# First two up-projection blocks of each MLP as a pair with a seven-product group, and every up pair's group moved to quad 3

## The reference

```
def sq_relu_mlp(h, w_up, w_down):
    return jnp.square(jax.nn.relu(h @ w_up)) @ w_down

for l in range(DEPTH):                      # DEPTH = 2
    ... attention, x = x + ...
    x = x + sq_relu_mlp(rms_norm(x, mlp_norm_g[l]), w_up[l], w_down[l])
```

## Time and profile before

| | |
|---|---|
| median of 3 runs | 1978.41 us |
| profiled execution | 1977.89 us |
| its span, first to last instruction | 1975.9 us |
| mean granted TensorE clock | 0.999 of full speed |
| busy: TensorE, its weight loads, VectorE, ScalarE | 100%, 83%, 85%, 62% |
| mean DMA rate | 212 GB/s |

### The profile page before, as it was taken

One profiled execution on the slowest core, in us unless ns is written; L12 is line 12 of the kernel. 1 busy time (PEld: TensorE's weight loads), 2 busy tenths in 40 slices (PEclk: granted clock), 3 DMA queues, 4 the chain that ended last, 5 costly groups with the idle time before them and its releaser, 6 DMA issues.

```text
span 1975.9 us, 24462 instructions
## 1 busy us (share of the span) xinstructions
PE 1966.4 (100%) x9068; PEld 1639.2 (83%) x9068; DVE 1679.9 (85%) x2053; ACT 1229.9 (62%) x1579; POOL 34.3 (2%) x45
## 2 busy tenths in 40 slices
PE   9999999999999999999999999999999999999998
PEld 7888888888888888888888998888888888888887
DVE  7789997878988998898886787977998898898886
ACT  6555555656667566656656665656566666666663
POOL 0000000000000000000000000000000000000000
PEclk9999999999999999999999999999999999999999
DMA  8655546766787587677666554676587678658663
GB/s 304 217 171 184 178 169 198 232 203 215 224 242 232 190 242 241 211 232 225 224 219 208 147 152 138 224 237 224 188 230 239 226 226 240 210 204 256 216 233 117
DMA packets 269406, 418.23 MB, mean 212 GB/s; under 512 B 18801, under 2 KB 88817, under 8 KB 269297
## 3 DMA queue, kind: packets, MB, share of 16 engines
q1 hardware_dynamic: 262800, 401.06, 62.2%
q0 software_dynamic: 3456, 12.58, 3.5%
q10 hardware_dynamic: 3040, 3.15, 0.5%
HBM read 379.00 MB, written 2.10 MB: 193 GB/s over the span
## 4 chain that ended last, share of the span: by engine, by line
PE 97%; issue 2%; DVE 0%; ACT 0%; POOL 0%; POOLq 0%; DVEq 0%; ACTq 0%
PE acc L622 23%; PE acc L624 23%; PE acc L623 23%; PE side L821 3%; PE side L822 3%; PE side L820 3%; PE acc L820 3%; PE acc L822 3%; PE acc L821 2%; PE acc L642 2%; PE acc L643 2%; PE acc L644 2%; PE acc L980 1%; PE acc L982 1%; PE acc L981 1%
## 5 line engine op out<-in xcount | busy, mean ns | idle before, releaser
L1127 ACT ACTIVATE whi<-raw 128x1024 fp32r<-128x1024 f32 x556 | 570.1, 1045 | 319.6 <-PE acc L624 251.7
L1774 DVE TENSOR_TENSOR wlo<-raw,whi 128x1024 fp32r<-128x1024 f32 x556 | 659.1, 1204 | 108.8 <-ACT whi L1127 107.2
L622 PE MATMUL acc<-whi,opA 128*128 128x512 f32 (+2 forms) x1072 | 414.8, 387 | 0.0
L624 PE MATMUL acc<-whi,opA 128*128 128x512 f32 (+2 forms) x1072 | 414.0, 386 | 0.0
L623 PE MATMUL acc<-wlo,opA 128*128 128x512 f32 (+2 forms) x1072 | 413.8, 386 | 0.0
L622 PE MATMUL acc<-whi,opB 128*128 128x512 f32 x944 | 368.7, 391 | 0.0
L624 PE MATMUL acc<-whi,opB 128*128 128x512 f32 x944 | 367.6, 389 | 0.0
L623 PE MATMUL acc<-wlo,opB 128*128 128x512 f32 x944 | 367.3, 389 | 0.0
L624 PEld LDWEIGHTS acc<-whi,opA 128*128 128x128 f32 x1072 | 201.3, 188 | 40.3
L622 PEld LDWEIGHTS acc<-whi,opA 128*128 128x128 f32 x1072 | 201.3, 188 | 40.1 <-issue 0.3
L623 PEld LDWEIGHTS acc<-wlo,opA 128*128 128x128 f32 x1072 | 201.4, 188 | 40.0
(11 more groups left out here) (385 smaller groups left out, 2824.6 us busy)
## 6 DMA issues: line engine op xcount, KB each, us to landing
raw<-in_w_up SPq DMA_DIRECT2D x128, 1024.0 KB, 6.0
raw<-in_w_down SPq DMA_DIRECT2D x128, 1024.0 KB, 5.1
raw<-in_a_w_qkv SPq DMA_DIRECT2D x44, 1024.0 KB, 5.1
prob<-o_sb SPq DMA_DIRECT2D x168, 128.0 KB, 2.6
raw<-in_a_w_o SPq DMA_DIRECT2D x16, 1024.0 KB, 5.1
raw<-in_b_w_o SPq DMA_DIRECT2D x16, 1024.0 KB, 5.1
raw<-in_w_ukv SPq DMA_DIRECT2D x32, 256.0 KB, 4.1
xs<-junk POOLq DMA_DIRECT2D x12, 512.0 KB, 5.5
```

Of the source, the lines that this page charges most:

```text
L622: mm(o, a_hi, w_hi, start=start, stop=False)
L624: done = mm(o, a_lo, w_hi, start=False, stop=last and c == chunks - 1)
L1127: done = fn(whi[:, place:place + ch, 0:n], raw[:, r, c0:c0 + ch, 0:n], ACT.Copy)
L1774: done = tt_(wlo[:, place:place + ch, 0:n], raw[:, r, c0:c0 + ch, 0:n], whi[:, place:place + ch, 0:n].bitcast(F32), ALU.subtract)
```

## The change

The first two up blocks of each MLP become a pair, ("up", l, 0, 0), with a group of its own. The groups of all up pairs work on quad 3 (`opA` chunks 12 to 15) in place of quad 0, and the `x_forms` are made from those chunks. The later up pairs keep their order of slots, halves and forms; only which rows of the weights are loaded into which slot changes. The new first pair has another order than they: on TensorE six halves of block 0 (quads 0 to 2), four halves of block 1 (quads 0 and 1), the group, and then the last two halves of block 1 (quad 2).

More of the change, by code:

```diff
@@ L893, in up_pair @@
                     for hf in range(6):
-                        half_tok(b, hf, 1, chunks_of(opA, 4 + 2 * hf), first=hf == 0, uses=uses[1])
+                        half_tok(b, hf, 1, chunks_of(opA, 2 * hf), first=hf == 0, uses=uses[1])
                     shares_free(SHARE["up", l, q, i])
                     pe.wait_ge(form_lo, FORM_SETS * l + 2)
-                    seven(GROUP["up", l, q, i], b, 6, opA, 0, x_forms, uses[0], True, SHARED + ("B21", "T4"))
+                    seven(GROUP["up", l, q, i], b, 6, opA, 12, x_forms, uses[0], True, SHARED + ("B21", "T4"))
                     for hf in range(6):
-                        half_tok(b + 1, hf + 2, 0, chunks_of(opA, 4 + 2 * hf), first=hf == 0, last=hf == 5, uses=uses[0],
+                        half_tok(b + 1, hf + 2, 0, chunks_of(opA, 2 * hf), first=hf == 0, last=hf == 5, uses=uses[0],
                                  starts=(False, True))
-                for j in range(2):
-                    block_tok(B_MLP[l] + j, 1 - j, u[1 - j], opA, ready=None if j else opA_ready(v_in))
+                def up_first():
[12 more added lines that the diff above has]
+                        half_tok(b + 1, hf, 0, chunks_of(opA, 2 * hf - 4), last=hf == 7)
+                up_first()
                 up_pair(0, 1)
@@ L1441, in hid_high @@
                        ACT.Copy).then_inc(hid_hi, 1)
[L1443 to L1449, removed]
                 def turn_order(sums):
@@ L1550, in last_gains @@
                     act.dma_start(g_high, final_norm_g[D // 2:D].partition_broadcast(P)).then_inc(g_high_in, 16)
[L1552 to L1555, removed]
-                up_pair(0, 1, "plain")
+                def up_first():
[16 more added lines that the diff above has]
+                    split(b + 2, 2)
+                up_first()
+                up_pair(0, 1, "up")
                 for q in range(QUARTERS - 1):
@@ L2316, in sum_first @@
                     dve.wait_ge(shared_sums, 4 * SHARE["up", l, q, i] + 3)
-                    dve.wait_ge(sq_moves, 64 * (JB * (QUARTERS * l + q) + 2 * i))
+                    if l or q or i:
+                        dve.wait_ge(sq_moves, 64 * (JB * (QUARTERS * l + q) + 2 * i))
                     if q and i == 0:
@@ L2450, in up_pair @@
                         split(b + 2, hf)
-                body(B_MLP[l], {7: lambda: x_lo(v_in + JB - 1, G_MLP[l]), 8: lambda: stream_stats(2 * l + 1, True),
-                                9: x_form_sums})
-                body(B_MLP[l] + 1, {3: lambda: up_turn(0, 0), 4: lambda: form_low(x_forms, FORM_SETS * l + 1), 6: lambda: hid_low(0, 0)})
-                up_pair(0, 1, "plain")
+                def up_first():
[17 more added lines that the diff above has]
+                    split(b + 2, 2)
+                up_first()
+                up_pair(0, 1, "up")
                 for q in range(QUARTERS - 1):
```

## The result

The changed kernel took 1993.34 us (median of 6 runs, 1992.19 to 1993.79) against 1978.3 us before (6 runs): a ratio of 1.0076, 95% interval 1.0066 to 1.0087, slower by 15 us. Its profiled execution took 1993.43 us over a span of 1991.6 us, 15.54 us above that of before. The time is 1.6 us above the forecast of 1991.7.

A forecast was written before the change was run, and what follows sets the result against it. TensorE, without gaps, was taken as the bound. Per MLP 4.8 + 3.0 - 1.15 = 6.65 us, twice 13.3, on the profiled 1977.89 gives 1991.2; 0.52 more for the runs' median makes 1991.7, range 1985.0 to 1997.5.

The forecast's parts named there:

- The bound: TensorE runs matmul after matmul between the first blocks and the end, so any new wait is added in full.
- The gain of a group: On TensorE, each MLP swaps four halves (10.89 us) for a group (9.74 us): 1.15 us less.
- Up to the new group: VectorE delivers everything up to the new group in time, the tightest form by 0.4 us: counted as 0.
- The first stall: TensorE waits 4.8 us per MLP for VectorE's low part of the second half behind the new group.
- The second stall: In the next pair TensorE waits 2.3 us for low half 4 and 0.7 for half 5: 3.0 per MLP.
- the shared chain: `sum_first`'s start fixes both stalls; were the first shorter, the second would be longer by as much.
- the weight sum: VectorE's first weight sum of the next group, 14.76 us behind `sum_first`'s start, forecast to start at 435.8.
- the moves and the load: SyncE issues the next load behind four moves of the squares, 3.93 us behind the turn's start; it lands 6.33 later.
- the clock at 1.00 through both: Forecast sign: TensorE's granted clock stays at 1.00 through both stalls, costing nothing; this case, 1991.7, got 56 in 100.
- its fall: Rival: the clock halves in the first stall, one half taking 2.7 us more per MLP: 1997.1; 24 in 100.
- The later time that I drew from the page's rule: By the skill page's rule, half rate until a stretch of work, the time would come out above the forecast.

The follow-up runs named there:

- f3_rearranged: f2_early_copies with the pair (0, 1) reordered: low halves 4 and 5 ahead of the first weight sum, turn behind the second; 1975.49 us, ratio 0.9986.
- f1_quad3_only: The kernel before with only the existing groups and the forms moved to quad 3, first two blocks plain; 1978.16 us, ratio 1.0001.
- e1_low7_first: The changed kernel with the low part of block 1's last half ahead of the combination and `sum_first` on VectorE; 1994.69 us, ratio 1.0083.
- e2_load_first: The changed kernel with SyncE issuing the shared quad's load ahead of the four moves of block 0's squares in pair (0, 1); 1991.05 us, ratio 1.0062.
- e3_both: The changed kernel with the reorderings of e1_low7_first and e2_load_first together; 1983.17 us, ratio 1.0025.
- e4_kept_busy: The changed kernel with 20 matmuls whose results nobody reads put on TensorE in the first stall; 1994.51 us, ratio 1.0082.
- f2_early_copies: e3_both with copies waiting only for the last shared product, and the next block's first low half ahead of the combination; 1978.31 us, ratio 1.0001.
- f4_load_first_busy: e2_load_first with the 20 unread matmuls of e4_kept_busy in the first stall; 1989.26 us, ratio 1.0053.

## Why the prediction was right, point by point

**The bound.** TensorE's queue had no gap, so each wait was added in full. Right: the stretches hold all of the growth.

**The gain of a group**, 1.15 us, taken from the distance of starts and not from the recorded 0.39 us a matmul. Right: shown alone by f3_rearranged, 1.13 per MLP.

**Up to the new group.** No wait at the group, as reckoned. Right, with f1_quad3_only behind it for the other pairs.

**The first stall.** Copies 416.19, combination 418.27, `sum_first` 421.05, low half 422.18 were forecast, and 416.13, 418.24, 421.03, 422.16 came. That is close because each step could be read in a later pair and only had to be set behind the new group's end. (423.4 + 2.72 is 426.12 and not 426.15, where the block ends; nothing rests on the 0.03 us.)

**The second stall** and the shared chain. The mechanism was right (e1_low7_first, e2_load_first and e3_both), and the weight sum started at 436.05, forecast 435.8. In the second MLP the load took 7.31 us from issue (1349.11) to use (1356.42), inside the range of the earlier trace rows but above my 6.33. The size was off in the first MLP, 1.35 for 3.0 us, because of the next point. What decides the time is when the sum starts, counted from the stretch's start: forecast 56.81 us, measured 57.06 and 58.50. These 0.25 + 1.69 us are most of the 2.35 by which the excess, 15.65, exceeds the forecast 13.3. So the term that was too small is the moves and the load in the second MLP, and not the clock.

**The step that failed: the clock at 1.00 through both.** I gave its fall 24 in 100, as the first stall was a little shorter than the only one with a fall in the trace of before. It fell in both MLPs. The term was also priced in the wrong way: I added it to the waits (1997.1). The prediction's own sentence, that the two stalls share one chain and a shorter first one only lengthens the second, holds for the low clock too: what it took from TensorE ahead of the second wait, 2.1 and 2.0 us, came off that wait, and the stretch ended 34.8 us behind the turn as it does with the clock held. The runs agree: the six of the changed kernel have a mean granted clock from 0.995 to 0.997, and the one with the lowest, 0.995, is the shortest (1992.19 us). So the forecast came near although its clock was wrong, since that error costs nothing here; this part was luck. The fall costs time where nothing waits behind it (1.6 and 1.2 us in e2_load_first, by the estimate above) or where it comes behind the second wait (0.85 us in the first MLP of e4_kept_busy). The page of the Trainium skill that I named ("TensorE: Matmul & The Clock Gate", Part 1) had the direction of the clock right, and the return that no row of before showed is in the windows above: the granted clock averages 0.50 from 426 to 427 and 0.79 from 427 to 428, so it came back in that last stretch. The later time that I drew from the page's rule, above my forecast, is not what these falls brought.

**What stays open.** In the second MLP the excess is 1.5 us larger than in the first, and the moves' issue (3.31 for 2.62 us) and the landing (7.31 for 6.56) account for it; why they were slower there was not tried. The account of the clock rests on one profiled execution of each kernel, with the granted clock of the others beside it.

## What to carry to other kernels

Where one engine is the bound and has no gap, what a change takes from it is small and certain, and what it needs from the others has a place in their queues: compare the cover, here two halves behind the group where later pairs have six, with the length of the chain that must fit under it. Two waits on one chain do not add: taking away the first only hands the time to the second, so cut the chain at both ends, and look again for the next holder behind it. The same goes for time lost to a low clock ahead of a wait: read what it costs at the end of the chain, not where the matmuls are slow. Of a step that is moved, ask first what stands behind it in each in-order queue; three of the four steps that turned 15 us lost into 2.6 us won were only other orders of the same instructions; the fourth let the copies wait for less.

## What the runs showed of the hardware

The granted clock falls after shorter waits than I had thought. In the profiled executions it fell after all waits of 5.0 us from start to start (four, in the changed kernel and e2_load_first), after those of 4.35 and 3.56 us (e1_low7_first) and after all four of 2.27 us (e1_low7_first, e3_both): matmuls at 0.43 us followed. Of three between 2.6 and 2.9 us only one was followed by them (e4_kept_busy's first MLP; not its second, nor the second MLP of the changed kernel). And three of the ten executions of e3_both show a mean clock of 0.999, that is no such fall. So length alone does not decide. No fall followed the waits of 1.33 us and less that f2_early_copies and f4_load_first_busy have.

Nor does the fall come at one place. In e2_load_first the granted clock is down before the matmuls are back (a mean of 0.54 from 423 to 424, with the first matmul at 423.94). In e4_kept_busy the first matmul behind the wait starts at 440.72 and the first distance of 0.43 us only at 442.14, 1.4 us later. Each fall lasted for 6 to 12 such distances, so whoever looks at the clock during the wait alone can miss it.
